# Forty more modulation tiles computed as row products on VectorE inside the half-row up projections, none on TensorE, and a regrouped preparation of the recurrence

## The reference

```
for l in range(DEPTH):                                   # DEPTH = 2, N_MOD = 9
    ml = jnp.split(s_lat @ w_mod[l] + b_mod[l], N_MOD, axis=-1)
    mc = jnp.split(s_ctx @ w_mod[l] + b_mod[l], N_MOD, axis=-1)
    x = half_ffn(x, g_norm[l, 0], ml[0], ml[1], ml[2], ...)      # ctx too, with mc
    ... token mixing with ml[3..5], mc[3..5] ...
    x = half_ffn(x, g_norm[l, 2], ml[6], ml[7], ml[8], ...)

def half_ffn(h, g, shift, scale, gate, wg, wu, wd):
    return h + 0.5 * gate * swiglu(modulate(rms_norm(h, g), shift, scale), wg, wu, wd)
```

## Time and profile before

| what | us |
| --- | --- |
| median of 3 runs (3010.04 to 3015.83) | 3012.65 |
| the profiled execution | 3011.66 |
| its span in the trace | 3010.4 |
| PE busy in the span | 2894.4 |
| PEld busy | 2364.9 |
| DVE busy | 1609.2 |
| ACT busy | 614.1 |
| POOL busy | 37.5 |

### The profile page before, as it was taken

The page is one execution under the profiler, slowest core; times in us unless marked ns, Lnnn a source line. Parts: engine busy times, 40 slices in busy tenths (PEclk is TensorE's granted clock), DMA queues, the critical chain, the costliest instruction groups (busy, mean ns, idle before and its releaser), DMA issues.

```text
span 3010.4 us, 41500 instructions
## 1 busy us (share of the span) xinstructions
PE 2894.4 (96%) x17066; PEld 2364.9 (79%) x17066; DVE 1609.2 (53%) x3259; ACT 614.1 (20%) x1388; POOL 37.5 (1%) x60
## 2 busy tenths in 40 slices
PE   8988999998999999999998999999999999999999
PEld 7767788984888978888643458888878888765999
DVE  4367467435466466673314546665366663225675
ACT  1245221134221121000214520000020000224110
POOL 0000000020000000000000000000000000000000
PEclk9999999999999999999999999999999999999999
DMA  6551465662565633322303013432344323331444
GB/s 237 187 198 32 141 214 158 197 182 84 177 214 147 192 131 129 117 79 77 112 26 112 29 56 126 137 117 58 110 146 131 120 72 81 110 108 55 142 142 111
DMA packets 344496, 376.17 MB, mean 125 GB/s; under 512 B 8723, under 2 KB 283556, under 8 KB 343540
## 3 DMA queue, kind: packets, MB, share of 16 engines
q1 hardware_dynamic: 324788, 306.65, 32.8%
q10 hardware_dynamic: 17312, 61.55, 5.6%
q0 software_dynamic: 2208, 5.31, 0.9%
HBM read 372.44 MB, written 1.05 MB: 124 GB/s over the span
## 4 chain that ended last, share of the span: by engine, by line
PE 90%; DVE 5%; ACT 4%; issue 1%; DMA 0%; ACTq 0%; DVEq 0%
PE acc L135 75%; PE aux L135 14%; ACT sb_xn L283 1%; PE aux L2433 1%; ACT L272 0%; DVE sb_work L2159 0%; DVE sb_work L2156 0%; ACT sb_work L1958 0%; ACT sb_work L1960 0%; DVE sb_xn L259 0%; DVE sb_work L1661 0%; PE acc L1045 0%; ACT sb_rstd L274 0%; DVE sb_work L1938 0%; DVE sb_work L2170 0%
## 5 line engine op out<-in xcount | busy, mean ns | idle before, releaser
L135 PE MATMUL acc<-sb_xn,weights 128*128 128x256 f32 (+2 forms) x5184 | 1217.7, 390 | 22.3 <-DVE sb_xn L259 14.0
L135 PEld LDWEIGHTS acc<-sb_xn,weights 128*128 128x128 f32 x5184 | 946.7, 191 | 247.5 <-issue 125.2
L135 PE MATMUL acc<-sb_work 128*128 128x256 f32 (+1 forms) x1944 | 375.0, 346 | 0.0
L135 PEld LDWEIGHTS acc<-sb_work 128*128 128x128 f32 x1944 | 324.4, 191 | 34.7 <-issue 0.4
L135 PE MATMUL acc<-sb_work,weights 128*128 128x256 f32 (+2 forms) x1508 | 322.4, 361 | 3.2 <-DVE sb_work L1394 1.4
L135 PE MATMUL acc<-sb_big,weights 128*128 128x256 f32 (+1 forms) x1776 | 313.8, 333 | 3.9 <-DVE sb_work L1815 3.8
L135 PEld LDWEIGHTS acc<-sb_big,weights 128*128 128x128 f32 x1776 | 278.1, 191 | 30.6 <-issue 5.2
L135 PEld LDWEIGHTS acc<-sb_work,weights 128*128 128x128 f32 x1508 | 254.2, 191 | 50.5 <-issue 21.8
L1629 ACT COPY sb_work<-acc 128x256 f32<-128x256 f32 (+1 forms) x112 | 38.0, 339 | 690.2 <-PE acc L135 690.2
L1699 DVE TENSOR_TENSOR sb_work<-sb_work,acc 128x256 f32<-128x256 f32 (+1 forms) x112 | 42.6, 381 | 228.8 <-PE acc L135 228.8
L135 PE MATMUL aux<-sb_xn,sb_work 128*128 128x256 f32 (+1 forms) x704 | 152.2, 360 | 8.4 <-ACT sb_xn L283 8.4
(11 more groups left out here) (353 smaller groups left out, 2716.0 us busy)
## 6 DMA issues: line engine op xcount, KB each, us to landing
weights<-ffn_w_up SPq DMA_DIRECT2D x88, 1024.0 KB, 9.1
weights<-ffn_w_down SPq DMA_DIRECT2D x48, 1408.0 KB, 7.2
weights<-ffn_w_gate SPq DMA_DIRECT2D x44, 1024.0 KB, 5.4
sb_work<-w_mod_rows ACTq DMA_DIRECT2D x60, 512.0 KB, 6.2
sb_big<-w_mod_rows ACTq DMA_DIRECT2D x44, 512.0 KB, 4.8
weights<-w_mod SPq DMA_DIRECT2D x10, 2048.0 KB, 8.1
weights<-w_in SPq DMA_DIRECT2D x8, 2048.0 KB, 8.7
weights<-mix_w_in SPq DMA_DIRECT2D x6, 2048.0 KB, 12.5
```

The source lines that it names most:

```text
L135: return te.matmul(o, lhsT, rhs, start=start, stop=stop, skip_group_check=True)
```

## The change

The ten TensorE blocks and all that served them (`Fill`, `tensor_modulation`, `scalar_modulation`, `vector_modulation`, `sync_modulation`, the selector matrix) go. Their 40 tiles become rows of the three half FFNs: 34, 33 and 33 tiles instead of 20 each, still in steps 1 to 20. Step i now does the half-rows from `upto(i - 1)` to `upto(i)` with `upto(i) = 2 n i // 20`, three or four of them, the first half of them at the early place, the rest at the late one, and all of step 20's at the early place. ACT loads in step i the tiles up to `upto(i - 1) // 2 + 1`. In `vector_prepare` the multiplication by the inverse norm moves behind three others. TensorE gets 10 products of ones behind the low-rank products and 24 behind the bonus sum, ahead of the recurrence; the bank they write is not read.

```diff
-ROWS_EACH, ROWS_CONV = 20, FT
-MOD_BY_PE = [(0, 16), (0, 17)] + [(1, b) for b in (0, 1, 2, 3, 4, 5, 16, 17)]
+ROWS_HALF, ROWS_UNTIL, ROWS_CONV = (34, 33, 33), 20, FT
...
-            if ft == 0:
-                other.to(4)
-        other.to(5)
...
-            if 1 <= n < 7:
-                other.to(5 + n)
             if n == 5:
                 te.wait_ge(gate_read.sem, gate_read_at(1))
                 next(first)
+        te.wait_ge(acc_free[2].sem, scan_banks[2])
+        tensor_idle(10, acc[2])
...
-        ve.wait_ge(pd_unit.sem, pd_unit_at(0))
-        v_step.on(ve.tensor_tensor(kk, kk, rho, ALU.mult))
+        ve.wait_ge(pd_set.sem, pd_first_at(0))
         v_step.on(ve.tensor_tensor(kr[:, :, 1, :], r_, dd_next, ALU.mult))
         ve.wait_ge(pd_rk.sem, pd_rk.n)
         v_step.on(ve.tensor_tensor(k_, k_, di, ALU.mult))
+        v_step.on(ve.tensor_tensor(t1, aa2, di, ALU.mult))
+        ve.wait_ge(pd_unit.sem, pd_unit_at(0))
+        v_step.on(ve.tensor_tensor(kk, kk, rho, ALU.mult))
...
         for _ in first:
             pass
-        other.to(MOD_FIRST)
+        tensor_idle(24, acc[2])
...
+            self.upto = lambda i: 2 * n * i // ROWS_UNTIL
...
-            if F.rows and 2 <= i < ROWS_EACH:
-                scalar_rows_load(F.rows, i)
+            if F.rows and 2 <= i <= ROWS_UNTIL:
+                for t in range(F.rows.upto(i - 2) // 2 + 2, min(F.rows.upto(i - 1) // 2 + 2, F.rows.n)):
+                    scalar_rows_load(F.rows, t)
...
-            if F.rows and 1 <= i <= ROWS_EACH:
-                vector_row(F.rows, i - 1, 0)
-                if i == ROWS_EACH:
-                    vector_row(F.rows, i - 1, 1)
+            if F.rows and 1 <= i <= ROWS_UNTIL:
+                middle = (F.rows.upto(i - 1) + F.rows.upto(i) + 1) // 2 if i < ROWS_UNTIL else F.rows.upto(i)
+                for n in range(F.rows.upto(i - 1), middle):
+                    vector_row(F.rows, n // 2, n % 2)
+                if i == ROWS_UNTIL:
                     vector_rows_bias(F.rows)
...
-                if F.rows and 1 <= i < ROWS_EACH:
-                    vector_row(F.rows, i - 1, 1)
+                if F.rows and 1 <= i < ROWS_UNTIL:
+                    for n in range(middle, F.rows.upto(i)):
+                        vector_row(F.rows, n // 2, n % 2)
```

More of the change, by code:

```diff
@@ L506, in build, with tensor_hyena @@
     hy_bias_at = hy_bias.reserve(4)
-    def tensor_hyena(other):
-        other.to(2)
+    def tensor_hyena():
         te.wait_ge(filt_ready.sem, filt_ready_at(3))
@@ L612, in scalar_gate_input, with scalar_lora @@
         gd_moved.on(ac.copy(gd2, gd))
-    def scalar_lora(other, first):
+    def scalar_lora(first):
         ac.wait_ge(wad_set.sem, wad_set_at(1))
@@ L624, in scalar_lora, with tensor_lora @@
             lora_read.on(ac.activation(aa[:, g, :], aux[2 * (n % 2) + 1][:, 0:L], ACT.Sigmoid, bias=cols("a0", 1, g)))
-            if 1 <= n < 7:
-                other.to(5 + n)
             if n == 3:
                 next(first)
-    def tensor_lora(other, first):
+    def tensor_lora(first):
         te.wait_ge(up_in.sem, 48)
@@ L676, in build @@
     b0, b1 = acc[0], acc[1]
-    scan_banks = [acc_free[b].planned for b in range(2)]
-    sil_set, pick_set = signal("condition_silu_set"), signal("partial_picker_set")
-    sil_at, pick_at = sil_set.reserve(1), pick_set.reserve(1)
+    scan_banks = [acc_free[b].planned for b in range(3)]
     NP = CT
@@ L800, in scalar_prepare @@
         a_step.on(ac.activation(di, t0, ACT.Exp, scale=DECAY_C))
-        a_step.on(ac.activation(dd_next, t0, ACT.Exp, scale=-DECAY_C))
+        pd_set.on(ac.activation(dd_next, t0, ACT.Exp, scale=-DECAY_C))
         ac.wait_ge(pd_clamp.sem, pd_clamp_at(0))
@@ L918, in tensor_ahead @@
         yield
[L920 to L1003, removed]
     def tensor_scan_out(p):
@@ L1030, in build, with tensor_scan @@
     BY_IDENT = (3, 4)
-    def tensor_scan(p, other, ahead):
+    def tensor_scan(p, ahead):
         def times(out_bank, lhs, rhs_, start=None):
@@ L1168, in tensor_scan, with scalar_scan @@
                 sc_y.on(local_out((b0, b1), 1))
-    def scalar_scan(p, other, ahead):
+    def scalar_scan(p, ahead):
         for hp in range(2):
@@ L1221, in scalar_scan, with vector_scan @@
         sc_tc.on(ac.copy(tc[:, 1], b0[:, 0:128].rearrange("p (g t) -> p g t", g=2)))
-    def vector_scan(p, other, ahead):
+    def vector_scan(p, ahead):
         for hp in range(2):
@@ L1462, in build, with __init__ @@
     class ModRows:
-        def __init__(self, first, n=ROWS_EACH, cond=row_cond, tiles=row_tile, junk=row_junk):
+        def __init__(self, first, n, cond=row_cond, tiles=row_tile, junk=row_junk):
             self.first, self.n, self.silu_cond, self.tiles, self.junk = first, n, cond, tiles, junk
@@ L2591, in build @@
     ple1 = Ple(1, ffn1.x_ready)
-    half00 = HalfFfn(0, 0, 0, ple1.x_ready, extra=(ctx_in, 32), squares=area(big, FT * L, KT, T2), rows=ModRows(2 * ROWS_CONV))
+    half00 = HalfFfn(0, 0, 0, ple1.x_ready, extra=(ctx_in, 32), squares=area(big, FT * L, KT, T2), rows=ModRows(2 * ROWS_CONV, ROWS_HALF[0]))
     mix0 = Mixing(0, True, half00.x_ready, hooked=True)
-    half01 = HalfFfn(0, 1, 0, mix0.x_ready, squares=area(big, 0, KT, T2), rows=ModRows(72 + 24))
-    half10 = HalfFfn(1, 0, 0, half01.x_ready, squares=hook_sq, hooked=True, rows=ModRows(72 + 24 + ROWS_EACH))
+    half01 = HalfFfn(0, 1, 0, mix0.x_ready, squares=area(big, 0, KT, T2), rows=ModRows(2 * ROWS_CONV + ROWS_HALF[0], ROWS_HALF[1]))
+    half10 = HalfFfn(1, 0, 0, half01.x_ready, squares=hook_sq, hooked=True, rows=ModRows(2 * ROWS_CONV + sum(ROWS_HALF[0:2]), ROWS_HALF[2]))
     mix1 = Mixing(1, False, half10.x_ready, hooked=True)
@@ L2669, in scalar_program @@
         ac.wait_ge(const_in.sem, 64)
[L2670 removed]
         scalar_mix_in()
         scalar_gate_input()
[L2673 to L2674 removed]
+        scalar_hyena()
         first = scalar_prepare()
[L2676 to L2677 removed]
+        scalar_lora(first)
+        scalar_recurrence(first)
         scalar_group_norm()
```

73 lines of the change are left out of this document (17 added, 56 removed).

## The result

| what | us |
| --- | --- |
| the changed kernel, median of 20 executions (3013.47 to 3030.31) | 3022.55 |
| the kernel before on the same chip, median of 20 (3007.70 to 3020.41) | 3014.78 |
| ratio, with its 95% interval | 1.0027 (1.0019 to 1.0035) |
| the profiled execution after (before: 3011.66) | 3016.58 |

The changed kernel is slower, by 0.27%, some 8 us. The forecast was 3016; this ratio times the 3012.65 known then makes 3020.8.

The account below looks back on a forecast made before the run. PE, busy 96% of the span, was taken as the bound where others wait for it. 3011.66 - 17.7 + 11.6 + 4.1 + 5.1 = 3014.8 us; the profiled execution lay 1.0 below the median, so 3016, range 2999 to 3027.

Parts of the forecast that it names:

- forecast of "no change": Whole kernel: median between 3006.6 and 3018.7 us, chance 0.37; slower than that 0.31, faster 0.32.
- signs of being wrong: Row loads landing within 6.3 us of a step's product 1, product 4 waiting elsewhere, recurrence met before 162 or after 166.
- The held product 4: Up projections: in four steps a row tile lands late beside the weight pair and holds PE's product 4; 11.6 us lost.
- The six events in steps without a weight pair: Up projections: the row load runs alone, lands 5.97 us into the step, free by 0.3; no cost.
- Step 21: Product 7 starts 1.35 us late in each of three stages, behind step 20's four early half-rows; 4.1 us lost.
- Falls of the clock behind the held products: Up projections: PE's clock falls after three of four idle times, 1.7 us each; 5.1 us lost.
- The front: Ahead of the recurrence: its first product moves from 181.49 to 163.8; 17.7 us gained.
- Inside the recurrence: Removed pieces lay in waits for DVE, costed at nothing; without cover the gain would grow by some 6 us.
- Rival A: Up projections: DVE's slack absorbs the row loads, no clash stalls, only 4.1 us cost; 2999 us, chance 0.27.
- Rival A2: Up projections: stalls come but the clock does not fall, without the 5.1 us; 3010.6 us, chance 0.13.
- Rival B: Up projections: a second row load delays the first by up to 1.7 us in ten events; 3031 us, chance 0.14.
- Rival C: Ahead of the recurrence: 24 products of ones take 10.7 us, not 5.3, gain 12.3; 3021 us, chance 0.10.

Follow-up runs that it names:

- `no_ones`: The changed kernel without the 10 and the 24 products of ones on PE ahead of the recurrence; measured 3017.54 us, ratio 1.0009 to the kernel before.

## Why the prediction was right, and where it was off

The time lies in the range; the forecast of "no change" was on the wrong side of its bound by a little, which had the chance of 0.31. Of the prediction's signs of being wrong one came: PE met the recurrence at 166.69, "after 166".

- **The held product 4: right in place, cause and nearly in size.** Four steps, the four named; 9.5 us where 11.6 were summed. DVE worked its queue off in 3.8, not 4.03, and the landing in step 16 took 6.6 us, not 7.4, so PE waited 1.90 there and not 3.5; of the others two were 0.3 to 0.4 shorter than forecast and one 0.2 longer. The six events in steps without a weight pair cost PE nothing, as said: in step 9 of `half00` the tile was taken up at S + 5.5 and product 4 started in its turn.
- **Step 21: right.** 3.8 for 4.1.
- **Falls of the clock behind the held products: sized for the typical execution.** Three of four were taken; the first profile has two (granted clock 0.60 and 0.61 over 4 us behind them), the second three.
- **The front: 14.8 for 17.7, the term that was mis-sized.** The step that failed is, of the gate products, "So they start at 148.41 - 2.9 = 145.5": they started at 148.44. I took modulation's removed time off and did not ask what else those records did. They kept PE at work in DVE's two waits (a fall of 1.7 was behind them afterwards), and an activation of the condition, part of the same machinery, loaded the sine's table at 12.80 in ACT's idle time; I had listed what the change removes on PE, DVE and SP, but not that instruction on ACT. Inside the recurrence, where the removed pieces were costed at nothing and named as up to 6 us more, they gave 0.8: behind it, PE's first products at 336.93 stand 15.6 before those of the kernel before (352.56).
- **Rival A (the stalls don't come)** fell: the row load beside the weight pair in step 8 of `half01` landed 7.0 us behind its issue (1876.91 to 1883.91), twice the 3.5 of one alone, and those of the other three held steps 6.6 to 7.6. The Trainium skill, page "DMA: Bandwidth & Descriptors", Arbitration, says that each DMA engine takes turns between the queues it has work for. The prediction read out of it a landing in well under twice the time of one alone; that reading failed, and the measurement decides. Whether turns were taken no run shows.
- **Rival A2 (the stalls come, the clock stays)** fell: two falls behind the four held products in the first profile, three in the second.
- **Rival B (the second row load delays the first)** fell: in the steps with two row loads and no weight pair the first was taken up at S + 5.4 to 5.6, no later than one alone would.
- **Rival C (the products of ones at the lower clock)** fell: they took 5.52 for 5.3 forecast, with the clock at 1.00.

Sum of the profiled execution by these: -14.8, +9.5, +3.8, and two falls of about 1.6 behind held products make +1.7; the measured +4.9 leaves 3.2. Outside the front and the held products the first profile after has 14 pieces of low clock and that of before 11, which is up to 5.1 us and enough to cover it. The rest of the medians' 8 is not seen in this profile; the granted clocks of all executions, above, say that it is mostly clock.

## What to carry to other kernels

Work that is moved to an idle engine costs by where its data arrives, not by its load: write down for every step which buffer each instruction opens and when that load is issued, and look for the steps where a rounding rule opens one step too early. Changing a table of counts was worth 22 us here, more than the 14.8 that the move gained at the recurrence. When a filler is removed, ask of every instruction of it what it did beside its result: kept an engine busy in a wait, or loaded a table while nobody needed ACT. And since a wait may or may not be followed by a low clock, compare medians of many executions with the sums of one profile only within a few such pieces.

## What the runs showed of the hardware that was not expected

- TensorE's granted clock went missing in pieces of 1.7 us, or a multiple, in all eleven profiles (a short rest at the very end of a span aside). The same idle time was followed by one in one execution and not in the next: 2.01 us idle at 573 us with a fall in the first profile of the changed kernel and without in the second, 2.09 us at 1640 us the other way about.
- What a piece costs in time depends on who waits for PE: in `no_ones` five pieces (8.5 us) stand ahead of and in the recurrence, where DVE sets the pace, and the kernel was 3.3 us late behind it.
- Idle times of only 1.50 and 0.88 us, with 0.4 us of work between them, were followed by a fall in eight of nine profiles.
